# First FFN: the fourth weight sum of each pair of blocks by a plain load and a VectorE addition, in place of an accumulating GpSimd transfer

## The reference

```python
ffn = (jax.nn.silu(h2 @ w_gate[l]) * (h2 @ w_up[l])) @ w_down[l]
...
mod = (c_act @ w_ada[l] + b_ada[l])[:, None, :]
shift1, scale1, gate1, shift2, scale2, gate2 = jnp.split(mod, 6, axis=-1)
```

## Time and profile before

| what | value |
|---|---|
| median of 3 runs | 955.33 us |
| lowest and highest | 954.2 and 958.57 us |
| the profiled execution | 958.16 us |
| its span in the trace | 956.1 us |
| granted TensorE clock, mean | 0.994 of full |
| TensorE busy in the first FFN (204 to 390 us) | 184.16 of 186.00 us |
| VectorE busy there | 156.73 us |
| ScalarE busy there | 108.61 us |
| DMA engines' share there | 0.79 |

### The profile page before, as it was taken

One profiled execution on the slowest core, in us unless ns is written; L12 is line 12 of the kernel. 1 busy time (PEld: TensorE's weight loads), 2 busy tenths in 40 slices (PEclk: granted clock), 3 DMA queues, 4 the chain that ended last, 5 costly groups with the idle time before them and its releaser, 6 DMA issues.

```text
span 956.1 us, 15251 instructions
## 1 busy us (share of the span) xinstructions
PE 942.1 (99%) x6383; PEld 812.3 (85%) x6383; DVE 743.2 (78%) x841; ACT 540.4 (57%) x687; POOL 63.7 (7%) x60
## 2 busy tenths in 40 slices
PE   8999999999999999999999999999999999999997
PEld 5799888988878788999888888889999888888886
DVE  2699978878887887787669987777776668987874
ACT  3584467466546465634265664657655656655554
POOL 0000660000100000100000000010000000000000
PEclk9999979999999999999999999999999999999999
DMA  9877224766798878556536878778653464978761
GB/s 338 298 255 284 72 84 140 271 219 253 174 354 213 315 182 309 208 181 212 202 115 166 269 214 272 214 212 288 257 170 128 144 218 142 259 217 269 216 176 44
DMA packets 41555, 204.54 MB, mean 214 GB/s; under 512 B 3408, under 2 KB 5904, under 8 KB 25744
## 3 DMA queue, kind: packets, MB, share of 16 engines
q1 hardware_dynamic: 35024, 180.37, 52.0%
q0 software_dynamic: 5760, 22.05, 12.4%
q10 hardware_dynamic: 704, 1.17, 0.4%
HBM read 202.49 MB, written 1.07 MB: 213 GB/s over the span
## 4 chain that ended last, share of the span: by engine, by line
PE 88%; DVE 6%; ACT 2%; DMA 1%; issue 1%; POOL 1%; SPq 0%; DVEq 0%; POOLq 0%; ACTq 0%
PE bank L2179 44%; PE acc L2179 41%; PE bank L2830 2%; DMA X_inv<-stream 1%; DVE w_lo L1419 1%; POOL X_inv L839 1%; PE bank L2576 1%; ACT w_hi L933 0%; DVE scores L1443 0%; DVE XT L1725 0%; PE bank L2281 0%; PE acc L2281 0%; PE bank L2286 0%; PE bank L2453 0%; DVE qkT L1713 0%
## 5 line engine op out<-in xcount | busy, mean ns | idle before, releaser
L1419 DVE TENSOR_TENSOR w_lo<-raw,w_hi 128x2048 fp32r<-128x2048 f32 x125 | 284.5, 2288 | 51.0 <-ACT w_hi L933 50.7
L933 ACT ACTIVATE w_hi<-raw 128x2048 fp32r<-128x2048 f32 x125 | 237.4, 1911 | 66.1 <-PE acc L2179 41.5
L2179 PE MATMUL bank<-w_hi,h_parts 128*128 128x512 f32 x696 | 225.0, 393 | 0.0
L2179 PE MATMUL acc<-h_parts,w_hi 128*128 128x256 f32 x928 | 169.7, 285 | 1.3 <-DVE h_parts L1471 0.7
L2179 PEld LDWEIGHTS bank<-w_hi,h_parts 128*128 128x128 f32 x696 | 130.7, 188 | 29.7 <-DVE h_parts L1496 1.5
L2179 PEld LDWEIGHTS acc<-h_parts,w_hi 128*128 128x128 f32 x928 | 142.3, 188 | 5.7 <-DVE w_lo L1541 2.1
L2179 PE MATMUL bank<-w_lo,h_parts 128*128 128x512 f32 x348 | 135.6, 390 | 0.0
L2179 PE MATMUL acc<-h_parts,w_lo 128*128 128x256 f32 x464 | 130.6, 281 | 0.0
L2179 PE MATMUL acc<-w_hi,o_hi 128*128 128x512 f32 x296 | 117.3, 396 | 1.8 <-DVE w_lo L1419 1.8
L2179 PE MATMUL acc<-w_hi,o_lo 128*128 128x512 f32 x296 | 115.4, 390 | 0.0
L2179 PE MATMUL acc<-w_lo,o_hi 128*128 128x512 f32 x296 | 115.3, 390 | 0.0
(11 more groups left out here) (412 smaller groups left out, 1353.7 us busy)
## 6 DMA issues: line engine op xcount, KB each, us to landing
raw<-stream SPq DMA_DIRECT2D x141, 1024.0 KB, 5.1
t_tables<-stream SPq DMA_DIRECT2D x9, 1024.0 KB, 5.9
x_res<-stream SPq DMA_DIRECT2D x9, 1024.0 KB, 8.1
x_res<-stream POOLq DMA_DIRECT2D x9, 1024.0 KB, 8.7
t_tables<-stream POOLq DMA_DIRECT2D x9, 1024.0 KB, 10.5
raw<-stream SPq DMA_DIRECT2D x6, 512.0 KB, 10.5
AT<-stream SPq DMA_DIRECT2D x2, 1024.0 KB, 11.6
qkT<-stream SPq DMA_DIRECT2D x2, 1024.0 KB, 13.0
```

Of the source, the lines that this page charges most:

```text
L933: act.activation(split_tile((w_hi, w_hi2), w), split_source(w), ACT.Copy).then_inc(s.hi_ready, 1)
L1419: dve.tensor_tensor(split_tile((w_lo, w_lo2), w), split_source(w), split_tile((w_hi, w_hi2), w), ALU.subtract).then_inc(s.lo_ready, 1)
L2179: return pe.matmul(o, l, r, start=start, stop=stop, skip_group_check=True)
```

## The change

In the first FFN alone (f = 0) the gate's high half for product 6 is no longer added to `chain[0]` by GpSimd's second accumulating transfer. It is loaded plainly into the ring of raw buffers, as a load of its own, (0, "pair", q, 6), in LOADS. VectorE adds it to `chain[0]` in a new function, `add_high_gate`, called right behind `up_sum(f, q, 0)`, that is ahead of the accumulation of the modulation block and of the down block's low part. ScalarE's high part of product 6 waits for that addition. The other two FFNs keep their transfers. The rest of the diff recounts semaphores: `operands_added` now rises three times in each pair of the first FFN instead of twice, and `rows_added` once instead of twice.

```diff
         label = LABEL.get(w)
         if label in MODS_LATE:
             out.append(("mod", MODS_LATE[label]))
-        if kind_of(w) != "pair" or label[3] in (1, 4):
+        if kind_of(w) != "pair" or label[3] in (1, 4) or label[0] == 0 and label[3] == 6:
             out.append(("w", w))
     return out
 
...
 
             return COPIES * f + 4 + 2 * q + n
 
+        def sums_ahead(f):
+
+            return (0, 4 + 3 * N_PAIRS, 8 + 5 * N_PAIRS)[f]
+
+        def sum_point(f, q, n):
+
+            return sums_ahead(f) + 4 + (2 if f else 3) * q + n
+
+        def rows_point(f, q, n):
+
+            return 16 * (q if f == 0 else N_PAIRS + 2 * (N_PAIRS * (f - 1) + q)) + 16 * n
+
         def unit_count(f, unit, t):
 
             return TT * (N_UNITS * f + UNIT_OF[unit]) + t + 1
...
             def add_weights(f):
 
                 for q in range(N_PAIRS):
-                    pool.wait_ge(s.operands_added, pair_point(f, q, 1))
+                    pool.wait_ge(s.operands_added, sum_point(f, q, 1))
                     pool.dma_start(halves_of(chain[1]), quarter(f, q, 1, 1), accum_op=ALU.add).then_inc(s.rows_added, 16)
-                    pool.wait_ge(s.rows_added, 32 * pair_count(f, q) + 16)
+                    if f == 0:
+                        continue
+                    pool.wait_ge(s.rows_added, rows_point(f, q, 1))
                     pool.wait_ge(s.lo_ready, pair_tile(f, q, 3) + 1)
                     pool.dma_start(halves_of(chain[0]), quarter(f, q, 0, 1), accum_op=ALU.add).then_inc(s.rows_added, 16)
 
...
                 if kind_of(w) == "pair" and LABEL[w][3] not in (1, 4):
                     f, _, q, n = LABEL[w]
                     if n in (2, 3):
-                        act.wait_ge(s.operands_added, pair_point(f, q, n - 1))
+                        act.wait_ge(s.operands_added, sum_point(f, q, n - 1))
+                    elif f == 0 and n == 6:
+                        act.wait_ge(s.operands_added, sum_point(f, q, 3))
                     elif n:
-                        act.wait_ge(s.rows_added, 32 * pair_count(f, q) + (16 if n == 5 else 32))
+                        act.wait_ge(s.rows_added, rows_point(f, q, 1 if n == 5 else 2))
                     else:
                         act.wait_ge(side_landed[0], 16 * (pair_count(f, q) + 3))
                 else:
...
                 r = weight_load(pair_tile(f, q, 4))
                 dve.wait_ge(*landed_of(r))
                 dve.wait_ge(s.lo_ready, pair_tile(f, q, 2) + 1)
+                dve.tensor_tensor(chain[0], chain[0], raw[:, r % RING, :], ALU.add).then_inc(s.operands_added, 1)
+
+            def add_high_gate(f, q):
+
+                r = weight_load(pair_tile(f, q, 6))
+                dve.wait_ge(*landed_of(r))
+                dve.wait_ge(s.lo_ready, pair_tile(f, q, 3) + 1)
                 dve.tensor_tensor(chain[0], chain[0], raw[:, r % RING, :], ALU.add).then_inc(s.operands_added, 1)
 
             def gate_sum(f, q):
...
                     hid_low(f, a - 1)
                     products(q, 5)
                     up_sum(f, q, 0)
+                    if f == 0:
+                        add_high_gate(f, q)
                     made(("down", a - 1 if q < 2 else a - 2))
                     pair_product(f, q, 0)
                     up_sum(f, q, 1)
```

More of the change, by code:

```diff
@@ L1207, in mixed_high_parts @@
                 for i in parts:
-                    act.wait_ge(s.operands_added, COPIES * f + (1, 3, 4, 2)[i])
+                    act.wait_ge(s.operands_added, sums_ahead(f) + (1, 3, 4, 2)[i])
                     act.activation(mixed_high[:, i, :, :], mixed_parts[i], ACT.Copy).then_inc(s.pairs_copied, 1)
@@ L1923, in mix @@
                 dve.tensor_tensor(s3, s2, s3, ALU.subtract).then_inc(s.operands_added, 1)
-                dve.wait_ge(s.operands_added, COPIES * f + 2)
+                dve.wait_ge(s.operands_added, sums_ahead(f) + 2)
                 dve.scalar_tensor_tensor(out=s2, in0=s1, scalar=-1.0, in1=s2, op0=ALU.mult, op1=ALU.subtract).then_inc(s.operands_added, 1)
                 rows_of(f, s4, 0, 4)
-                dve.wait_ge(s.operands_added, COPIES * f + 3)
+                dve.wait_ge(s.operands_added, sums_ahead(f) + 3)
                 dve.scalar_tensor_tensor(out=s4, in0=s2, scalar=-1.0, in1=s4, op0=ALU.mult, op1=ALU.subtract).then_inc(s.operands_added, 1)
```

## The result

The changed kernel takes 973.09 us (median of 6 runs, 971.46 to 976.0), the kernel before 954.11 us in the same comparison (6 runs, 953.36 to 958.57): ratio 1.0199, interval 1.0185 to 1.0214, so 19.0 us slower (17.7 to 20.4). Forecast were 15.5 us and 970.8 us, in a range from 963.0 to 979.0.

The account below looks back on a forecast made before the run. TensorE was taken as the bound (busy 99% of the span), so only its waits in the first FFN counted. Delays of 6.6 + 6.6 + 2.3 = 15.5 us on the 955.33 us median gave 970.8 us, range 963.0 to 979.0.

Parts of the forecast that it names:

- The direction and the place: Slower: TensorE already waits for low parts at down(2), down(5), down(7), gate and up 5 and 8; VectorE work ahead delays it.
- the first term: VectorE's addition ahead of the accumulations starts down(2), down(5) and down(7) 2.4, 2.3 and 2.3 us late: 7.0 us.
- The ring: One more load puts up(5) and up(8) third of three transfers: gate and up 5 and 8 each 6.6 us late, addition included.
- The removed transfer: GpSimd's accumulating transfer, for which ScalarE idles before product 6: its removal credited with nothing, at most 2.7 us.
- The landing of the new load: In SyncE's queue at gate(5)'s old place: lands in 4.7 us, delaying the first pair's addition 0.1 us, the others nothing.
- Rival B: TensorE's clock also falls behind the waits at gate and up 5 and 8: up to 10.2 us more, middle 975.9 us; 0.25.
- the sign that the prediction named: In the changed kernel's trace, a granted clock of 0.50 in the first FFN would show that the clock falls as well.
- A: Only the addition costs; transfers ahead of up(5) and up(8) do not hold them up: 8.1 us, 963.4 us; chance 0.10.
- C: Not slower: slack before the down blocks hides the addition and earlier product 6 gives up to 2.7 us, 952.6 us; 0.05.
- D: The wait before down(7) or the FFN's end is looser than read, a third of the sum lost: 965.6 us; 0.10.

Follow-up runs that it names:

- The addition alone with a full clock: Kernel before, with the low parts of down(2), down(5), down(7) formed twice and 7, 5, 7 matmuls of zeros ahead of those blocks: 961.18 us, 1.0068.
- the addition alone: Kernel before, with one more VectorE instruction per pair of the first FFN: low parts of down(2), down(5), down(7) formed twice, no load changed: 964.67 us, 1.0104.
- the kernel kept busy: Changed kernel with 10, 5 and 8 matmuls of zeros on TensorE ahead of down(2), down(5), down(7): 976.77 us, 1.0224 against the kernel before.
- the ring alone: Changed kernel without its addition and without GpSimd's accumulating transfer, the gate's high half loaded but left out of product 6: 967.86 us, 1.0136 against the kernel before.
- the load alone: Changed kernel without its addition, GpSimd's accumulating transfer kept, VectorE waiting for the new load without using it: 976.53 us, 1.0222 against the kernel before.

## Why the prediction was right, and where its sizes were off

**The direction and the place** were right: TensorE waits for low parts at five places, and what was put ahead of them arrived there in full. The addition alone with a full clock gave 7.0 us, the first term to the tenth; in the change the three starts came to 8.3 us, by the waits for the new load.

**The ring** was right: gate and up 5 waited for up(5), third of three transfers. That this is a matter of SyncE's own queue was not: x_res from GpSimd's queue held up(5) as long (8.1 us). Without any addition the waits were 3.5 and 4.4 us; in the change they are partly replaced by a slower down block, with the same sum (7.3 and 6.3 us for the two pairs, 6.6 and 6.6 forecast).

**The removed transfer**, credited with nothing: right in the sum, wrong in the reason. It ended no wait, but its absence is what lets the new load land in 5.8 us, where it took 9.2 us with the transfer kept.

**The landing of the new load** was mis-sized: 4.7 us to land and 0.1 us of waiting were assumed, it took 5.8 us and VectorE waited 1.14 us. The row of 4.7 us was the first load of a group of three and not of one by itself. The new load had none beside it but down(2)'s, which landed 0.3 us after its issue. In the third pair it took 5.1 us. Why it took longer in the first stays open.

**The clock** is the larger miss. Rival B put the falls behind the waits before gate and up 5 and 8 and added them whole. In the profiled execution they came behind down(2) and down(5), some 1.6 us each, and were made up by shorter waits for up(5) and up(8). So that execution fits the sum without them: 16.8 us against 15.5. By the sign that the prediction named, a clock of 0.50 in the first FFN, B is in all the same. The median, 973.09 us, lies just above the band that the forecast had for itself (969 to 973) and below the middle of B (975.9). That the falls met waits that hid them was not foreseen: here the forecast had luck. The runs of the change had mean clocks of 0.989 to 0.994, those of before mostly 0.997 to 1.000; a run at 0.989 took 974.9 and 976.0 us, one at 0.994 took 971.5 and 972.2. The 2.2 us between 16.8 and 19.0 come together like this. Some 0.3 us lie behind the last matmul. The profiled execution of before, 958.16 us less the 3.1 us by which its early stretch is the longer, is 955.1 us; the median of before lies 1.0 us below that. And the median of the change lies 0.9 us above its profiled execution, 972.17 us; its runs are slower the lower their mean clock. No run of the change at 0.989 was profiled, so where those lose their time was not shown. The nearest trace is the one with x_res in GpSimd's queue, at 0.990 and 974.12 us: nothing at 1.2 GHz ahead of the FFN, and 4.3 us lost in it to falls that found no wait to hide in. That such falls cost time shows as well in the addition alone and in the kernel kept busy (2.0 and 2.6 us at gate and up).

**A, C and D** are settled: A by the addition alone and by the ring alone, C by the waits, D since each of the starts came later than its forecast sum and nothing behind the FFN gave time back.

## What to carry to other kernels

Cost an instruction that is put ahead of a wait of the bounding engine at its full length, then look up which transfers its load displaces: here the displaced loads cost as much as the addition. Then ask what the new idle time does to the clock, and whether a later wait would hide that loss. Measuring one half of a change by itself is only clean if what the other half removes is removed too.

## What the runs showed of the hardware

- TensorE's clock fell to 1.2 GHz at or behind waits of 2.35 us (the change, down(5)) to 4.5 us (kept busy, gate and up 5) in a stretch of dense matmuls, a loss of 1.4 to 2.9 us each. It did not fall behind every such wait: in the change not behind 3.46 us before down(7). Matmuls of zeros in the wait kept the clock up (1.00 against 0.98 in the first FFN, with the addition alone).
- A plain load of 1 MB beside an accumulating transfer of 1 MB took 9.2 us (the load alone) where it took 5.8 us without (the change).
- A load of 1 MB took 8.1 us behind one load of its own queue and one of GpSimd's, as it did behind two of its own queue (up(5), in the kernel with x_res from GpSimd's queue and in the change).
